# Moving rows between SBUF partitions by DMA instead of by matrix products in a state-space loop

## The reference

```
xBC = silu(conv4(xBC));  dt = softplus(dt_raw + dt_bias);  a = -exp(a_log) * dt
cs  = cumsum(a)                                   # one row of T numbers for each of 32 heads
for each head h:                                  # state-space product, 64 channels a head
    decay[s, t] = exp(cs[h, t] - cs[h, s])  for s <= t, else 0
    y[:, t]     = sum_s (C[t] . B[s]) * decay[s, t] * dt[s] * x[s, :]  +  d_skip[h] * x[t, :]
y = group_norm(y * silu(z))
# rotation (a quarter of each head's rows) of 8 query tiles, 8 index-query tiles, 3 key tiles
q = q * cos + partner(q) * sin                    # partner exchanges the two halves of the rotated rows
# then an indexer picks 64 keys of each query, attention over them, w_out, residual
```

## Time and profile before

| what | before |
|---|---|
| median of 3 runs | 3596.31 us (3595.64 to 3598.92) |
| the profiled execution | 3597.59 us, its span 3595.8 us |
| PE busy | 3515.2 us, 98% of the span |
| DVE busy | 1504.8 us, 42% |
| ACT busy | 486.2 us, 14% |
| mean granted TensorE clock | 0.994 of full speed |
| the two loops, in the span | from about 2117 to 2292 us and from about 3103 to 3270 us |

### The profile page before, as it was taken

How to read it: one execution, slowest core, us unless ns; L and a number is a source line. 1 busy time by engine, 2 the same in 40 slices (tenths; PEclk the granted TensorE clock), 3 DMA queues, 4 the chain that set the end, 5 groups by cost and what they waited for, 6 DMA issues and landing times.

```text
span 3595.8 us, 47831 instructions
## 1 busy us (share of the span) xinstructions
PE 3515.2 (98%) x20239; PEld 2942.6 (82%) x20239; DVE 1504.8 (42%) x2787; ACT 486.2 (14%) x1113; POOL 26.9 (1%) x58
## 2 busy tenths in 40 slices
PE   7999999999999999999999999999999999999999
PEld 6888888888888998888888877777778888878877
DVE  1426531333466452513336636425233366363343
ACT  1012200011011101011001012112120010121111
POOL 1000000000000000000000000000000000000000
PEclk9999999999999999999999999999999999999999
DMA  6443244443444203644435433333444454332431
GB/s 204 140 142 117 94 141 140 145 131 106 134 136 141 72 4 127 223 133 133 148 109 160 140 117 94 92 119 106 152 139 144 120 165 140 117 117 83 135 123 71
DMA packets 436064, 454.45 MB, mean 126 GB/s; under 512 B 25227, under 2 KB 412736, under 8 KB 435328
## 3 DMA queue, kind: packets, MB, share of 16 engines
q1 hardware_dynamic: 433408, 444.68, 39.1%
q0 software_dynamic: 2144, 5.32, 0.4%
q10 hardware_dynamic: 320, 1.70, 0.1%
HBM read 449.58 MB, written 2.10 MB: 126 GB/s over the span
## 4 chain that ended last, share of the span: by engine, by line
PE 95%; DVE 2%; ACT 1%; DVEq 1%; issue 0%; ACTq 0%; DMA 0%; POOL 0%; POOLq 0%
PE bank L1798 31%; PE bank L284 18%; PE bank L380 9%; PE bank L1930 9%; PE bank L411 5%; PE bank L313 3%; PE bank L1996 3%; PE bank L1485 3%; PE bank L1045 3%; PE bank L297 2%; PE bank L1902 1%; PE bank L1983 1%; PE bank L1855 1%; PE bank L1883 1%; PE bank L1956 0%; PE bank L779 0%
## 5 line engine op out<-in xcount | busy, mean ns | idle before, releaser
L1798 PE MATMUL bank<-xnT,ring 128*128 128x272 f32 (+2 forms) x4992 | 1133.6, 389 | 0.0
L1798 PEld LDWEIGHTS bank<-xnT,ring 128*128 128x128 f32 (+1 forms) x4992 | 941.4, 189 | 188.5 <-issue 11.7
L284 PE MATMUL bank<-xnT,ring 128*128 128x272 f32 (+1 forms) x2816 | 633.2, 388 | 1.6 <-ACT wk L799 1.0
L284 PEld LDWEIGHTS bank<-xnT,ring 128*128 128x128 f32 x2816 | 534.7, 190 | 99.7 <-issue 3.3
L380 PE MATMUL bank<-xnT,ring 128*128 128x256 f32 x1536 | 343.5, 383 | 0.7 <-ACT wk L1219 0.7
L380 PEld LDWEIGHTS bank<-xnT,ring 128*128 128x128 f32 x1536 | 290.8, 191 | 41.3 <-ACT wk L1219 1.1
L1930 PE MATMUL bank<-G,ring 128*128 128x272 f32 (+1 forms) x1024 | 238.7, 388 | 0.0
L1930 PEld LDWEIGHTS bank<-G,ring 128*128 128x128 f32 x1024 | 192.8, 190 | 36.9 <-issue 3.6
L411 PE MATMUL bank<-G,ring 128*128 128x256 f32 x768 | 169.9, 385 | 9.6 <-DVEq L941 4.8
L411 PEld LDWEIGHTS bank<-G,ring 128*128 128x128 f32 x768 | 148.2, 193 | 31.1 <-DVEq L941 5.2
L460 DVE RECIPROCAL G<-G 128x272 f32<-128x272 f32 (+3 forms) x25 | 149.4, 5977 | 2.0 <-issue 0.3
(11 more groups left out here) (532 smaller groups left out, 2910.0 us busy)
## 6 DMA issues: line engine op xcount, KB each, us to landing
ring<-in_w_in SPq DMA_DIRECT2D x156, 2048.0 KB, 8.2
ring<-in_w_out SPq DMA_DIRECT2D x32, 2048.0 KB, 8.4
ring<-in_w_br SPq DMA_DIRECT2D x12, 2048.0 KB, 8.5
ring<-in_w_out SPq DMA_DIRECT2D x16, 1024.0 KB, 10.7
G<-in_x POOLq DMA_DIRECT2D x2, 1024.0 KB, 9.0
wk<-in_pool_w POOLq DMA_DIRECT2D x2, 1024.0 KB, 9.0
ring<-in_w_in SPq DMA_DIRECT2D x4, 512.0 KB, 5.7
out<-G SPq DMA_DIRECT2D x8, 256.0 KB, 2.4
```

Source lines behind the costliest of these rows:

```text
L284: mm = pe.matmul(bank[j][:, first:T], ring[:, s, k, j * P:(j + 1) * P], rhs[:, k, first:T], start=(k == 0), stop=(k == KT - 1))
L1798: mm = pe.matmul(out_, ring[:, s, k, c:c + m], xnT[:, k, first:T], start=(k == 0), stop=(k == KT - 1))
```

## The change

Both kinds of helper product leave PE. The sums' rows are now spread by a DMA that reads one row of `cs` 128 times and writes it to one of four buffers in SBUF (`steps_at`, a part of `merged` that is free here); the partner rows of a rotation tile are moved by two DMAs of 16 rows (kind "A") or four of 8 rows (kind "I") into one of three buffers (`partner`, in `wk`). ACT issues all of them, two pairs ahead of their use: `move_steps` behind its wait for `b2_in` and ahead of the exponential, `move_partner` behind its wait for `sq_in` and ahead of the square. DVE waits for seven new semaphores (`cs_out0` to `cs_out3`, `swap_out0` to `swap_out2`) in place of `work_full`. The sign of the exchange is put into the sine table. The subtractions now read SBUF. Three clearings of `partner` (128x272 each) are added on DVE ahead of the loop. The group means and the attention gate move to other, free places of the same size.

```
         def layers_pe(pe):
...
-                        def broadcast(h):
-
-                            po = 32 * (h % 2)
-                            hot = eye[po:po + 32, po + h:po + h + 1].to_broadcast([32, P])
-                            pe.matmul(use()[:, m0:T], hot, cs_two[po:po + 32, 0, m0:T], start=True, stop=True)\
-                              .then_inc(work_full, 1)
-
                         for pair in range(4):
-                            for hh in range(2):
-                                broadcast(8 * gr + 2 * pair + hh)
...
                             mm.then_inc(work_full, 1)
-                            rope(4 * gr + pair)
...
-                output_products(W8)
-                for n in range(16, len(ROPE_TILES)):
-                    rope(n)
-                    output_products(W8)
+                output_products(4 * W8)
...
+            def move_steps(h):
+
+                i = h % 4
+                src = cs[h:h + 1, 0, m0:T].unsqueeze(1).to_broadcast([1, P, T - m0])
+                act.dma_start(steps_at[i][:, m0:T], src).then_inc(S[f"cs_out{i}"], 16)
+
+            def move_partner(n):
+
+                dst, j, kind = ROPE_TILES[n]
+                r0 = first_row(dst, m0)
+                half = 16 if kind == "A" else 8
+                for at in ((0,) if kind == "A" else (0, 64)):
+                    for to_, from_ in ((at, at + half), (at + half, at)):
+                        act.dma_start(partner[n % 3][to_:to_ + half, r0:T], dst[from_:from_ + half, j, r0:T])\
+                           .then_inc(S[f"swap_out{n % 3}"], 16)
...
+                    if t == W8 + 2:
+                        for h in range(4):
+                            move_steps(h)
...
+                    if half == 0:
+                        for n in range(2):
+                            move_partner(n)
                     for pair in range(8):
-                        for d in decay:
+                        for hh, d in enumerate(decay):
                             wait("b2_in")
+                            if 8 * half + pair + 2 < 16:
+                                move_steps(16 * half + 2 * pair + 4 + hh)
                             act.activation(d[:, m0:416], d[:, m0:416], ACT.Exp)
...
                         wait("sq_in")
+                        if 8 * half + pair + 2 < 16:
+                            move_partner(8 * half + pair + 2)
                         act.activation(G[:, 2 + half, pair, m0:T], G[:, 4 + half, pair, m0:T], ACT.Square).then_inc(S["sq_done"], 1)
...
+                move_partner(16)
                 for j in range(1, 4):
                     tile(kv_[:, j, :], P)
+                    if j == 1:
+                        act.drain()
+                        move_partner(17)
                 act.wait_ge(proj_full, tiles["act"].go(2))
                 act.activation(kv_[:, 4, :], bank[0][:, 0:T], ACT.Copy).then_inc(proj_free, 2)
+                act.drain()
+                move_partner(18)
...
                 def rope(n):
...
-                    t, d = rope_row[:, r0:T], dst[:, j, r0:T]
-                    v.tensor_tensor(t, full()[:, r0:T], sin[:, r0:T], ALU.mult).then_inc(work_free, 1)
-                    v.tensor_tensor(d, d, cos[:, r0:T], ALU.mult)
+                    t, d = partner[n % 3][live, r0:T], dst[live, j, r0:T]
+                    wait(f"swap_out{n % 3}", 32 if kind == "A" else 64)
+                    v.tensor_tensor(t, t, sin[live, r0:T], ALU.mult)
+                    v.tensor_tensor(d, d, cos[live, r0:T], ALU.mult)
...
+                for t in partner:
+                    v.memset(t, 0.0)
                 v.drain()
                 v.nop().then_inc(S["b2_pe"], 1)
...
-                                b = full()
+                                wait(f"cs_out{h % 4}", 16)
+                                b = steps_at[h % 4]
```

More of the change, by code:

```diff
@@ L118, in rope_tables @@
     out = []
-    swaps = []
     for d in (128, 64):
@@ L124, in rope_tables @@
         ang = np.arange(T, dtype=np.float32)[None, :] * inv.astype(np.float32)[:, None]
-        cos, sin, swap = np.ones((d, T), np.float32), np.zeros((d, T), np.float32), np.zeros((d, d), np.float32)
+        cos, sin = np.ones((d, T), np.float32), np.zeros((d, T), np.float32)
         cos[:half] = cos[half:rot] = np.cos(ang)
-        sin[:half] = sin[half:rot] = np.sin(ang)
-        for i in range(half):
-            swap[half + i, i] = -1.0
-            swap[i, half + i] = 1.0
-        n = P // d
-        out += [np.tile(cos, (n, 1)), np.tile(sin, (n, 1))]
-        swaps.append(np.kron(np.eye(n, dtype=np.float32), swap))
-    return np.concatenate(out + swaps, axis=1).astype(np.float32)
+        sin[:half] = -np.sin(ang)
+        sin[half:rot] = np.sin(ang)
+        out += [np.tile(cos, (P // d, 1)), np.tile(sin, (P // d, 1))]
+    return np.concatenate(out, axis=1).astype(np.float32)
 STACKS2 = []
@@ L1645, in build @@
         tables = fc[:, FC["blk"][0]:FC["blk"][0] + 4 * T]
-        swaps = lev8[:].bitcast(F32)
         cosA, sinA, cosI, sinI = (tables[:, T * i:T * (i + 1)] for i in range(4))
-        swapA, swapI = swaps[:, 0:P], swaps[:, P:2 * P]
-        rope_row = flat(wk)[:, 3 * L_END:3 * L_END + T]
-        means = G[:, 2:4].rearrange("p a (b c) t -> p (a b) c t", c=4)[:, :, 0, :]
+        partner = [flat(wk)[:, 3 * L_END + T * i:3 * L_END + T * (i + 1)] for i in range(3)]
+        steps_at = [rest[:, 4 + i, :] for i in range(4)]
+        means = rest[:, 0:4, :]
         exps = tok[:, 0:W8 * T].rearrange("p (a t) -> p a t", t=T)
@@ L1663, in build @@
         q_, iq_, kv_ = g[1], g[0], g[6]
-        attn, a_gate = g[2], rest
+        attn = a_gate = g[2]
         kv_k, kv_i, iw_row = kv_[:, 0:2], kv_[:, 4:5], cs_two[32:48, 1, :]
@@ L1677, in begin, with first_row @@
             return META if layer == LAST else 0
+        def first_row(dst, m0):
+            return 0 if dst is kv_k or dst is kv_i else m0
         def vec2(name, n, at=0):
@@ L1747, in layers_pool @@
             pool.dma_start(meta2, ins["meta_tokens_2"]).then_inc(S["meta2_in"], 16)
-            pool.dma_start(tables, ins["rope"][:, 0:4 * T]).then_inc(S["rope_in"], 16)
-            pool.dma_start(swaps, ins["rope"][:, 4 * T:]).then_inc(S["rope_in"], 16)
+            pool.dma_start(tables, ins["rope"]).then_inc(S["rope_in"], 16)
             for layer in range(LAYERS):
@@ L1848, in layers_pe @@
                 mm.then_inc(work_full, 1)
-                if layer == 0:
-                    wait("rope_in", 32)
-                def rope(n):
-                    dst, j, kind = ROPE_TILES[n]
-                    r0 = 0 if dst is kv_k or dst is kv_i else m0
-                    pe.matmul(use()[:, r0:T], swapA if kind == "A" else swapI, dst[:, j, r0:T], start=True, stop=True)\
-                      .then_inc(work_full, 1)
                 def group_sums(gr):
@@ L2306, in steps @@
                     v.drain()
-                    v.tensor_copy(cs_two[32:64, 0, :], cs[:, 0, :])
                     v.tensor_copy(cs[:, 1, 16:T], cs[:, 0, 16:T])
@@ L2346, in rope @@
                     dst, j, kind = ROPE_TILES[n]
-                    cos, sin = (cosA, sinA) if kind == "A" else (cosI, sinI)
-                    r0 = 0 if dst is kv_k or dst is kv_i else m0
-                    t, d = rope_row[:, r0:T], dst[:, j, r0:T]
-                    v.tensor_tensor(t, full()[:, r0:T], sin[:, r0:T], ALU.mult).then_inc(work_free, 1)
-                    v.tensor_tensor(d, d, cos[:, r0:T], ALU.mult)
+                    r0 = first_row(dst, m0)
+                    live, cos, sin = (slice(0, 32), cosA, sinA) if kind == "A" else (slice(0, 80), cosI, sinI)
+                    t, d = partner[n % 3][live, r0:T], dst[live, j, r0:T]
+                    wait(f"swap_out{n % 3}", 32 if kind == "A" else 64)
+                    v.tensor_tensor(t, t, sin[live, r0:T], ALU.mult)
+                    v.tensor_tensor(d, d, cos[live, r0:T], ALU.mult)
                     v.drain()
@@ L2361, in layers_dve @@
                     v.memset(d[:, 416:L_END], 0.0)
+                for t in partner:
+                    v.memset(t, 0.0)
                 v.drain()
                 v.nop().then_inc(S["b2_pe"], 1)
+                if layer == 0:
+                    wait("rope_in", 16)
                 b = full()
@@ L2395, in layers_dve @@
                                     at = SSD_AT[i] + p0 - t0
-                                    df = v.tensor_scalar(d[0:n, at:at + p1 - p0], b[0:n, p0:p1],
-                                                         cols2[0:n, 3 + a, h:h + 1], 0.0, ALU.subtract, ALU.min)
-                                df.then_inc(work_free, 1)
+                                    v.tensor_scalar(d[0:n, at:at + p1 - p0], b[0:n, p0:p1],
+                                                    cols2[0:n, 3 + a, h:h + 1], 0.0, ALU.subtract, ALU.min)
                                 to("b2_in")
```

3 lines of the change are left out of this document (1 added, 2 removed).

## The result

The changed kernel takes **3617.35 us** (median of five runs, 3613.99 to 3620.83), the kernel before, timed beside it, 3596.31 (3593.83 to 3604.39). The ratio is 1.0055, with a 95% interval of 1.004 to 1.007: slower, by 21 us. Forecast were 3561 us, and 3550 to 3578 as the range.

The account below looks back on a forecast made before the run. PE, busy 98% of the span, was taken as the bound. Products removed from it save 39.5 us, less 1.6 at loop starts and 2.4 in the middles: 35.5 off 3596.3, giving 3561 us, range 3550 to 3578.

Parts of the forecast that it names:

- What is hidden, and by what: Spread-row DMAs in the loops: landings of 8.2 to 10.7 us at most, hidden because wanted some 15 us after issue.
- third rival: Spread rows land late: on one DMA engine, two a pair take 17.4 us, time about 3840; 3 in 100.
- What is put on ACT: DMA issues ahead of exponentials and square: 0.44 us each, 0 to 0.66 as ends; only the second exponential's delays the turn.
- second rival: Issues cost x us each, ACT becomes the bound, turn 7.21 + 2x; 13 in 100 faster, 7 slower including late landings.
- The turn of PE: One pair inside the groups: PE's turn falls from 9.77 to 8.46 us in layer 1, 9.26 to 8.00 in layer 2.
- DVE and ACT keep up: Inside the groups: DVE and ACT need 8.15 us against PE's 8.46, and 7.71 against 8.00, so PE stays the bound.
- The subtractions: On DVE, reading SBUF instead of a bank: 0.059 us less each, six a pair, 0.35 us a pair.
- The middle of the loop: Four issues ahead of the square delay the copies: turn 17.62 us against 16.41, 1.2 us lost a layer, 2.4 in all.
- The start of the loop: PE waits for three new clearings on DVE, 0.24 us each, plus 0.09: 0.8 us lost a layer, 1.6 in all.
- The late products: Exchange products leaving PE late: six save 0.47 or 0.44 us each, 2.7; behind the last pair about 1.2, both layers.

Follow-up runs that it names:

- seventh kernel: Changed kernel with the spread rows read from HBM, exchange DMAs issued behind the square and the middle's copies, and no clearings of the partner buffers: 3557.12 us, ratio 0.9883.
- eighth kernel: Changed kernel with only the issue order changed, exchange DMAs behind the square and in the middle behind the copies: 3601.78 us, ratio 1.0011.

## Why the prediction was wrong

**The step that failed is "What is hidden, and by what".** It bounded the landing of a spreading transfer by 8.2 and 10.7 us, from transfers out of HBM, and asked only whether it is ready for its own reader 15 us later. In latency this was nearly right: the landings are 7.1 to 18.8 (the longest ahead of the loops), 10.2 in the median, and DVE's wait for them isn't what holds PE. What it left out is capacity. While transfers read from one row queue, they land about 5.2 us apart (136 KB, 27 GB/s over all 16 engines together; the profile's slices show just 27 wherever nothing else moves), two a pair are 10.4, and the turn is to be 8.46. No lead helps against this: the backlog grows by about 2 us each turn until the next issue is held. The prediction did use the right formula, two transfers a pair against the turn, in its third rival, but only for a transfer on one DMA engine, and gave it 3 in 100.

**Capacity alone doesn't make the kernel slower, though.** A loop has 28 such transfers; at 5.2 us they are 146 us, and the loop before took 158.6. The kernel with the exchange on PE shows what this limit allows: its first loop takes 146.6, and its 28 transfers have landed 141.5 us after the first of their issues, since edges and middle, 12.6 us longer than inner turns together, let the queue catch up. With the exchange issued by POOL the loop is 150.0. The changed kernel needs 164.3. What lies between is the second step that failed, "What is put on ACT": an issue was to have a price of its own, whatever is under way, and a held one keeps ACT from the square, the copies and the exponentials.

**"What is put on ACT"** took 0.44 an issue, 0.66 as the end. Unheld they are 0.33 from HBM, 0.48 to 0.54 from one or 128 SBUF rows, and mostly 0.51 to 0.75 for the exchange: the term was a little small and harmless in the turn. Held ones are up to 5.1. The second rival ("the issues are dear") had the place right, between DVE's release and the exponential, and its signs in the profile: PE waits for DVE, DVE for ACT. It had the reason wrong: it read an issue as having a fixed price x, and the price is the backlog's. By its formula x = 1.5 gives 3621, but that it comes near 3617 is chance: most issues take 0.5 to 0.75, and the held ones up to several times 1.5.

**The turn of PE** is right to the hundredth: 8.46 and 8.00, wherever the transfers are quick. So is that DVE and ACT keep up: with 0.52 an issue they need, by the prediction's own terms, an estimated 8.06 + 0.52 - 0.41 = 8.17. **The subtractions** gained 0.41 a pair (2.29 for twelve against 2.70), forecast 0.35. The Trainium skill's page VectorE: DVE Perf Modes (section The TRN2 errata), by which the prediction worked out 131 ns each and 0.8 in all, doesn't give the measured gain here: one of 128 columns went from 341 to 281 ns.

**The middle of the loop** was forecast at 17.6 with four issues of 0.44. Unheld it is 19.6: 0.9 from issues of 0.66, and about 1 from the clock, which the prediction didn't have at all. In the changed kernel it is 22.2: of the further 2.6, 1.7 are a held issue again (4.37 for the four).

**The start of the loop** was forecast at 0.8 a layer. The clearings take 0.87 instead of 0.72; the other 1.1 is what goes with the clock.

**The sum of the parts that were not broken.** With the source in HBM and the diff's order the time is 27.6 below the kernel before, forecast 35.5. The two middles (2.0 and 2.3 too dear, as each was to lose 1.2 and lost 3.2 and 3.5) and the two starts (1.0 and 0.8) make 6.1 of the 7.9 missing. The late products gave 1.8 a layer, forecast 1.95 (1.2 for both layers behind the last pair and 2.7 for the six). With both places mended the gain is 41.1 us. That this lies near the forecast's 3561 is partly luck: the seventh kernel has another source, another order and no clearings, and 3.8 us of its gain aren't explained.

**What stays open.** That one row gives only 27 GB/s to 16 engines is shown by what changes when the source does, but not what in the memory limits it. Two rows read by all 16 engines, once neighbours and once far apart, would tell a limit per row, one shared by neighbours and a price on repetition from each other; the form at hand gives two rows to two engines, and no kernel with another was run. What the clock costs in the changed kernel's loops was not measured apart, beyond the edge above. And where a held issue waits, in the queue or at the engines, no row says.

## What to carry to other kernels

For a transfer that recurs in a loop, compare its time of service, and not only its landing, with the turn: a landing may be hidden, and the queue still fall behind. The DMA that repeats one SBUF row over all partitions moved 27 GB/s here, with 16 DMA engines on it; the same row from HBM, written there once a layer, landed in 3.1 us instead of 10.5. And put issues behind the work for which another engine waits, on an in-order engine that has both: the same four issues cost 3.9 us ahead of the copies, and nothing behind them (a middle of 15.69, and 15.73 in the kernel that has no exchange issues at all).

## What the runs showed of the hardware

- Transfers of one SBUF row read 128 times (136 KB) land about 5.2 us apart when they queue, 27 GB/s, with 16 DMA engines taking part; 32 rows land after 2.7 us, 128 rows after 2.1, one row in HBM after 3.1. By the packets' times two neighbouring rows on two engines moved no more than one row on 16 (an estimated 32 and 33 GB/s), and eight 56.
- An issue on ACT was held for up to 5.1 us once about two and a half such transfers were outstanding, whatever its own size, while POOL's queue took its issues in 0.5 in the same stretch. Other queues feel it too: the loops' weights, issued by SP, landed after 20.7 us in the median, and after 8.1 before (both over 2137 to 2265 us), though PE never waited for them in the first loop.
- At the start of the loops the clock of PE fell to its lower level behind waits of 2.68 to 2.70 us, in all ten kernels with the clearings, and kept 1.00 behind 1.81 and 1.82 in the other three. There this more than doubles the price of 0.87 us of clearings. The length of the wait alone doesn't tell: elsewhere the clock fell behind waits of 1.95 (changed kernel, 3131.88) and 2.41 us (2169.30), and kept 1.00 behind one of 2.84 (eighth kernel, 3194.13).
